# A gate matrix written by accumulating scatters in place of one-hot products, in a PEER expert layer

## The reference

```
qry = (xt @ w_query).reshape(PEER_BLOCK, PEER_HEADS, 2, PEER_KEY_DIM)
s1, s2 = scores of the two halves of qry against keys1, keys2      # 128 each
v1, i1 = lax.top_k(s1, PEER_TOPK);  v2, i2 = lax.top_k(s2, PEER_TOPK)
cand_s = all 16 x 16 sums v1 + v2;  top_s, pos = lax.top_k(cand_s, PEER_TOPK)
idx = i1 * 128 + i2 of the chosen pairs
gate = softmax(top_s)
act = gelu(einsum('td,thkd->thk', xt, expert_u[idx]))
out = einsum('thk,thkd->td', gate * act, expert_v[idx])
```

## Time and profile before

| what | us |
|---|---|
| median of 3 runs | 4345.73 (4339.46 to 4351.4) |
| the profiled execution, its own time | 4333.4 |
| span of that execution, first to last instruction | 4331.6 |
| PE busy | 3828.7 |
| DVE busy | 2677.1 |
| POOL busy | 1476.8 |
| ACT busy | 911.4 |

### The profile page before, as it was taken

The page is one execution under the profiler, slowest core; times in us unless marked ns, Lnnn a source line. Parts: engine busy times, 40 slices in busy tenths (PEclk is TensorE's granted clock), DMA queues, the critical chain, the costliest instruction groups (busy, mean ns, idle before and its releaser), DMA issues. The chain is left out here.

```text
span 4331.6 us, 43998 instructions
## 1 busy us (share of the span) xinstructions
PE 3828.7 (88%) x16016; PEld 2836.8 (65%) x16016; DVE 2677.1 (62%) x5272; ACT 911.4 (21%) x1953; POOL 1476.8 (34%) x1456
## 2 busy tenths in 40 slices
PE   8889999967999999994798899999669999999937
PEld 7647788856766666651685478788557666666516
DVE  4865116568567666777658651175685676667775
ACT  2252202146200000000123522021461000000001
POOL 6102000023355455556370020000243555555663
PEclk9899999989999999997898999999899999999968
DMA  3001233358899999999620102333589999999996
GB/s 101 30 32 37 84 136 119 125 191 285 338 391 399 405 391 410 375 410 401 252 80 30 39 30 94 126 127 133 192 292 348 388 402 404 391 410 374 409 384 258
DMA packets 300550, 1063.83 MB, mean 246 GB/s; under 512 B 41648, under 2 KB 75056, under 8 KB 274992
## 3 DMA queue, kind: packets, MB, share of 16 engines
q0 software_dynamic: 147456, 536.94, 32.2%
q1 hardware_dynamic: 119312, 488.44, 29.6%
q10 hardware_dynamic: 33568, 35.65, 2.3%
HBM read 1025.27 MB, written 35.65 MB: 245 GB/s over the span
## 5 line engine op out<-in xcount | busy, mean ns | idle before, releaser
L2022 POOL DMA_INDIRECT u_rows<-in_peer_u,idx_all x512 | 659.1, 1287 | 1654.8 <-DVEq L1925 933.5
L1629 PE MATMUL bank<-v_tile,shared 128*128 128x512 f32 x2048 | 904.5, 596 | 15.3 <-DVE shared L1972 15.2
L1945 DVE SCALAR_TENSOR_TENSOR x<-v_rows,act_w,x 128x1024 f32<-128x1024 f32 x512 | 657.7, 1285 | 210.8 <-DMA v_rows<-in_peer_v,idx_all 180.7
L2022 POOL DMA_INDIRECT v_rows<-in_peer_v,idx_all x512 | 582.3, 1137 | 456.1 <-DVE x L1945 340.9
L1629 PEld LDWEIGHTS bank<-v_tile,shared 128*128 128x128 f32 x2048 | 391.5, 191 | 466.9 <-issue 443.0
L1933 DVE CUSTOM_DVE_ANT_0 u_rows<-u_rows,h 128x1024 f32<-128x1024 f32 x512 | 606.4, 1224 | 103.3 <-DMA u_rows<-in_peer_u,idx_all 102.2
L1617 PE MATMUL bank<-hT,bT 128*128 128x256 f32 x2048 | 452.5, 379 | 0.0
L1617 PEld LDWEIGHTS bank<-hT,bT 128*128 128x128 f32 x2048 | 388.4, 190 | 72.0 <-issue 22.0
L1520 PE MATMUL bank<-hT,ring 128*128 128x256 f32 x1536 | 340.9, 383 | 14.2 <-PEq L150 14.2
L1520 PEld LDWEIGHTS bank<-hT,ring 128*128 128x128 f32 x1536 | 293.5, 192 | 56.5 <-issue 15.8
L1799 ACT ACTIVATE shared<-bank 128x512 f32<-128x512 f32 x128 | 76.2, 595 | 1023.4 <-PE bank L1629 948.7
(11 more groups left out here) (356 smaller groups left out, 5143.9 us busy)
## 6 DMA issues: line engine op xcount, KB each, us to landing
v_tile<-in_peer_v SPq DMA_DIRECT2D x256, 512.0 KB, 7.1
ring<-in_w_in_panels SPq DMA_DIRECT2D x76, 1024.0 KB, 4.8
bT<-in_peer_ut SPq DMA_DIRECT2D x128, 512.0 KB, 7.5
ring<-in_peer_w_query SPq DMA_DIRECT2D x32, 1024.0 KB, 4.9
aT<-in_peer_ut SPq DMA_DIRECT2D x64, 512.0 KB, 6.7
sT<-in_peer_ut SPq DMA_DIRECT2D x64, 512.0 KB, 7.1
gates<-dense_gates SPq DMA_DIRECT2D x32, 1024.0 KB, 10.6
ring<-in_ple_w_gate SPq DMA_DIRECT2D x24, 1024.0 KB, 7.9
```

The lines of the kernel that those rows point to most:

```text
L1629: ins = mm(acc[t][part][:, :], act_pair[p % AHEAD][:, at:at + P], v_tile[:, e % DENSE, part * 512:part * 512 + 512], start=(e == 0), stop= ...
L1945: stt(out=m.x[:, 2 + t, :], in0=vr[:, n % RINGS, :], scalar=act_w[:, p % 4, i:i + 1], in1=m.x[:, 2 + t, :], op0=ALU.mult, op1=ALU.add).the ...
L2022: nc.gpsimd.indirect_dma_start(out=rows[:, n % RINGS, :], out_offset=None, in_=table, in_offset=bass.IndirectOffsetOnAxis(ap=idx_all[:, t, ...
```

## The change

The `hot` steps and `slots` are gone. The gates are put into the DRAM matrix one by one instead.

In `phase_attend`, POOL sets a tile of zeros and SP issues 8 DMAs of 2 MB that clear this layer's cells; SP waits for them before the phase ends. In `choose`, for the first half, DVE computes the flat number of the cell (second index, first index, token) with two fused instructions and a conversion; `token` (two columns of token numbers) is made by three small DVE instructions at the start of the tail. For each head, POOL issues 32 indirect DMAs (`scatter`) of 128 single elements, each of which adds its element to its cell (`compute_op=ALU.add`), 256 in a layer. Several heads of one token can choose the same cell, so POOL waits for all adds of one head to land before it issues those of the next. Seven heads' adds come before the first fetch in POOL's program, the last head's 32 lie among the fetches of chunks 0 to 3, eight to a chunk. SP waits for all 256 before it reads the first gates.

The order changes too: four `pre` pairs come before chunk 0, two more before each of chunks 0 to 3; `values` is spread over chunks 5 to 55, and `DENSE_END` is 56. The layout of a token's cells in DRAM loses its blocks of 32 tokens; each read of the gates is as large as before.

```diff
 # phase_attend, SP
             Panels(m, s, []).stream(sp, input_panels(io, layer, "deltanet"))
+            sp.wait_ge(s.zeros_set, 1)
+            n = KEYS // ZERO_PARTS
+            for k in range(ZERO_PARTS):
+                sp.dma_start(io.gates[layer, :, n * k:n * (k + 1), :].rearrange("p e t -> p (e t)").rearrange("p (r z) -> p r z", z=ZEROS),
+                             over(zeros[:, :].unsqueeze(1), (P, n * HALF_T // ZEROS, ZEROS))).then_inc(s.cells_cleared, 16)
+            sp.wait_ge(s.cells_cleared, 16 * ZERO_PARTS)
...
 # tail_order
-    pairs = 0
-    for q in range(QUADS):
-        order.append(("hot", q))
...
-    for c in range(HOT_CHUNKS, CHUNKS + 2):
-        goal = min(PAIRS_ALL, -(-(c - HOT_CHUNKS + 1) * PAIRS_ALL // (DENSE_END - HOT_CHUNKS)))
+    for c in range(CHUNKS + 2):
+        order += [("pre", p) for p in range(UPFRONT + 2 * c, min(UPFRONT + 2 * c + 2, AHEAD))]
+        goal = max(0, min(PAIRS_ALL, -(-(c - VALUES_FROM + 1) * PAIRS_ALL // (DENSE_END - VALUES_FROM))))
...
 # SP, values(0)
-                    for k in range(2):
-                        sp.wait_ge(stored[k], 16 * 4)
+                    sp.wait_ge(m.scattered, 16 * SCATTERS * PEER_HEADS * (layer + 1))
...
 # DVE, choose, part 3, first half of the tokens
+                        step.step(stt(out=chosen[:, 0], in0=chosen[:, 0], scalar=float(HALF_T), in1=over(token.unsqueeze(2), (P, 2, TOPK)),
+                                      op0=ALU.mult, op1=ALU.add))
+                        step.step(stt(out=chosen[:, 0], in0=chosen[:, 1], scalar=float(KEYS * HALF_T), in1=chosen[:, 0], op0=ALU.mult, op1=ALU.add))
+                        step.mark(ts(cell_all[:, :, some], chosen[:, 0], float(layer * CELLS), None, ALU.add))
...
 # POOL
+            def scatter(n):
+                t, col = n % SCATTERS // TOPK, n // SCATTERS * TOPK + n % TOPK
+                if n % SCATTERS == 0:
+                    pool.wait_ge(s.first_chosen, n // SCATTERS + 1)
+                    if n:
+                        pool.wait_ge(m.scattered, 16 * (SCATTERS * PEER_HEADS * layer + n))
+                nc.gpsimd.indirect_dma_start(
+                    out=cells, out_offset=bass.IndirectOffsetOnAxis(ap=cell_all[:, t, col:col + 1], axis=0),
+                    in_=cell_gate[:, t, col:col + 1], in_offset=None, compute_op=ALU.add,
+                ).then_inc(m.scattered, 16)
+
+            late = SCATTERS * (PEER_HEADS - 1)
+            for n in range(late):
+                scatter(n)
             for n in range(RINGS):
                 fetch(n, s.u_free, u, tables[0], m.u_landed)
...
+                if c < LATE_CHUNKS:
+                    for n in range(SCATTERS // LATE_CHUNKS):
+                        scatter(late + c * SCATTERS // LATE_CHUNKS + n)
```

More of the change, by code:

```diff
@@ L710, in _ @@
             Panels(m, s, []).stream(sp, input_panels(io, layer, "deltanet"))
+            sp.wait_ge(s.zeros_set, 1)
[4 more added lines that the diff above has]
+            sp.wait_ge(s.cells_cleared, 16 * ZERO_PARTS)
+        @block.gpsimd
+        def _(pool):
+            nc.gpsimd.memset(zeros[:, :], 0.0).then_inc(s.zeros_set, 1)
         @block.scalar
@@ L1315 @@
 AHEAD = 12
-EARLY = 6
-STORE_T = 32
-BLOCKS = HALF_T // STORE_T
+ZEROS = 512
+ZERO_PARTS = 8
 OCT = 8
 OCT_PAIRS = OCT // 2
-QUADS = HALF_T // 4
-HOT_CHUNKS = 8
-DENSE_END = 58
+CELLS = P * KEYS * HALF_T
+SCATTERS = 2 * TOPK
+LATE_CHUNKS = 4
+UPFRONT = 4
+VALUES_FROM = 5
+DENSE_END = 56
 def tail_order():
@@ L1347, in tail_order @@
     order += [("choose", PEER_HEADS, part) for part in range(4)]
-    order += [("score", 1, 1), ("slots",)]
+    order += [("score", 1, 1)] + [("pre", p) for p in range(UPFRONT)]
     beside = {}
@@ L1587, in score @@
                 ins.then_inc(s.act_filled, 1)
[L1589 to L1605, removed]
             def pre(p):
@@ L1662, in embedded @@
                 ins.then_inc(s.vec_filled, 1)
-            parts = {"gate": gate, "mix": mix, "out": out, "norm": norm, "query": query, "score": score, "slots": slots, "hot": hot, "pre": pre,
+            parts = {"gate": gate, "mix": mix, "out": out, "norm": norm, "query": query, "score": score, "pre": pre,
                      "values": values, "turn": turn, "embedded": embedded}
@@ L1750, in score @@
                 elif half or head >= 4:
-                    act.wait_ge(s.dsel_ready, head + 5 if half else head - 3)
+                    act.wait_ge(s.first_chosen, head + 5 if half else head - 3)
                 bank = banks.take()
@@ L1823, in _ @@
             parts = {"gate": gate, "mix": mix, "norm": norm, "query": query, "score": score, "choose": choose, "chunk": chunk,
-                     "slots": slots, "hot": hot, "pre": pre, "embed": embed, "turn": turn, "embedded": embedded}
+                     "pre": pre, "embed": embed, "turn": turn, "embedded": embedded}
             for what, *n in order:
@@ L1833, in _ @@
             tt, ts, stt = nc.vector.tensor_tensor, nc.vector.tensor_scalar, nc.vector.scalar_tensor_tensor
+            spread = hit[:, 0:KEYS // TOPK, :].rearrange("p a n -> p (a n)")
+            step.mark(tt(spread, m.c("ident"), m.c("iota"), ALU.mult))
+            step.settle()
+            step.mark(nc.vector.tensor_reduce(token[:, 0:1], spread, AX_X, ALU.add))
+            step.settle()
+            step.mark(ts(token[:, 1:2], token[:, 0:1], float(P), None, ALU.add))
+            step.settle()
             def mix(half, pair):
@@ L1917, in choose @@
                     for a in range(2):
-                        step.mark(nc.vector.tensor_reduce(chosen[:, a] if half else dsel[:, a, :, some], h5[:, a], AX_X, ALU.add))
+                        step.mark(nc.vector.tensor_reduce(chosen[:, a], h5[:, a], AX_X, ALU.add))
                     v.wait_ge(s.exp_done, 2 * k + 2)
@@ L2003, in embedded @@
                 tt(xs, xs, ple_sig[:, n, at].rearrange("p (t c) -> p t c", t=len(UNITS[unit])), ALU.add).then_inc(s.ple_added, 1)
-            parts = {"mix": mix, "out": out, "norm": norm, "choose": choose, "chunk": chunk, "hot": hot, "values": values, "add": add,
+            parts = {"mix": mix, "out": out, "norm": norm, "choose": choose, "chunk": chunk, "values": values, "add": add,
                      "embed": embed, "turn": turn, "embedded": embedded}
```

80 lines of the change are left out of this document (18 added, 62 removed).

## The result

The changed kernel takes 4609.8 us (median of four runs, 4609.2 to 4614.6) and the kernel before 4347.4 (four runs, 4339.5 to 4351.4): a ratio of 1.061, 95% interval 1.059 to 1.063. It is 262 us slower. The forecast was 4289, and the range ended at 4560.

What follows compares the result with a forecast made beforehand. PE and DMA were taken as full together from 1160 to 1900 us, with slack only before `values`. Starting `values` 59.5 us earlier minus 31 for moved chunks gives 28.5 per layer, 57 in both: 4289 us, range 4225 to 4560.

Steps and rivals of the forecast that it cites:

- The step that failed: POOL's adds: each priced like an indirect fetch, one every 1.24 us in the choosing stage, 1.49 in the chunks.
- POOL's start: Choosing stage, layer 1: head 0 ready at 682.9 plus about 0.6 us of new DVE instructions, so adds start at 683.5.
- 224 adds to the first fetch: Seven heads of 32 adds on POOL, 42.7 us each with landing, put the first fetch at 982.4 instead of 919.77.
- From the first fetch to the last add: POOL in chunks 0 to 3: 70 fetches and adds at 1.49 us, 104.3 us, to 1086.7.
- From there to the product: Landing 3 us, gates to DVE's product 5.5, PE 1.3 later, 3 for lower clock: `values` starts at 1099.5.
- Rival (a): Adds cost POOL more than fetches; gain gone at 1.35 us, with 0.47 us more busy time 4529 us; chance 0.30.
- The landing: POOL's wait behind each head for its last add to land before the next head: taken as 3 us.
- The end: Dense stretch and behind: three chunks, 12.6 MB, move into full DMA time, costing 31 us per layer of the 59.5 gained.
- The clearing: Attention stage: clearing writes 16.8 MB, needs 42 us at 397 GB/s, covered by some 120 us of idle DMA; cost nothing.
- (c): Dense stretch: the three chunks cost 17 us each, giving back 51 of 59.5 us per layer; 4329 us; chance 0.14.
- (d): Layer's end: gain kept in full, extra chunk hidden and the rest where PE idled 52.94 us; 4227 us; chance 0.12.
- (b): DMA engines drain adds slower than POOL issues them, 1.36 us each, perhaps 2.7; about 5030 us; chance 0.06.

Runs made afterwards that it cites:

- forms kernel: A kernel of its own, POOL issuing 24 indirect DMAs of each form and none of the layer's work: median 1549 ns with the add flag, 962 without.
- the split kernel: Against the kernel before: tile 0's gates by adds, tile 1's by `hot` steps; 4273.3 us, ratio 0.983; three variants moved `DENSE_END` or the start of `values`, 4219.7 to 4247.5.
- a spacer: Changed kernel with single-element gathers in place of adds, plus a POOL memset of 384 columns behind each gather: 4440.3 us, ratio 1.021.

## Why the prediction was wrong

**The step that failed** is "It also handles 128 rows, so the nearest row is the fetch, and I take 1.24 us for it". The nearest row was near in what POOL handles and not in how. The add takes 1.55 us and 0.30, 1.85 in place of 1.24. The forms kernel shows the 0.59 by itself, whatever is moved, and the runs with half of the adds and with none show what it does. The prediction's terms for the start of `values` against the trace of after:

- POOL's start: 683.5 predicted, 686.85 measured: +3.3. Of that 2.9 is there before the choosing: the DeltaNet phase's first product starts at 259.27 in place of 256.39.
- 224 adds to the first fetch: 298.9 us predicted (982.4 - 683.5), 444.9 measured: +146. Of that 224 x (1.85 - 1.24) = 137 is the form; the landings took 14 beyond the usual gap (15.8 us in six waits) in place of 7 x 3 = 21; of the other 17, 6 are adds longer than 1.55 us and most of the rest four gaps of 1.9 to 3.2 us for which the profile names no releaser.
- From the first fetch to the last add: 104.3 predicted, 117.1 measured: +13, which is 32 adds by 0.3 to 0.4 each.
- From there to the product: 12.8 predicted, 14.2 measured: +1.4. From the last add to the read of the gates 1.4 us, where I had 3; from there to DVE's product 6.4, where I had 5.5; and PE 6.4 behind it, where I had 1.3 and 3, since the first `v_tile` loads stand behind SP's new wait, which I left out.

Together +163.5: 1263.0 in place of 1099.5. In the kernel as a whole the adds come to 487 us, the difference to the kernel without them.

**Rival (a)** names the mechanism and its break-even, 1.35 us, and the prediction's own test ("If the adds are 1.4 us apart or more") decides it. It had 0.30, and its price was a guess: 0.47 us more busy time, where the mean of 1.60 is 0.66 more. With that, 4289 + 512 x 0.66 = 4627, 17 over what was measured. The upper bound of the add, 2.18, was sound and its end, 4770, was named; the range was then cut at 4560 because the fetch seemed near. There the range failed, not at the bound.

**What the sum did not ask** is how many adds fit. It had POOL behind DVE by its own numbers, the first fetch at 982.4 against 919.77, and charged that; but it took all 256 adds of a layer as given. The first 128 cost 14 us a layer and the other 128 cost 229; this is what the split kernels use.

**The landing** is near: the waits behind a head are 2.28 us at the border shown above and 2.45 on average, where I took 3. The Trainium skill, "DMA: Bandwidth & Descriptors", "Anatomy of one DMA — SWDGE (gpsimd) path", has a fixed 2.0 us for the setup and completion of a DMA. By that figure, 32 adds issued 1.85 us apart and done one after the other would leave 32 x 0.15 + 2.0 = 6.8 us behind a head (an estimate). The measured 2.45 bears out the overlap.

**The end** is right in size and half right in reason. By the bytes the three chunks were to cost 31 us per layer; the tail grew by 35.9, from 1013.3 to 1049.2, and in every kernel with after's order it is within about 2 us of that (1047.1, 1050.3, 1048.8), wherever `values` started. But the split kernel has a tail of 1045.7 with the dense result added after chunk 56 and 1027.9 after 58, with the same bytes. So there about half of the term comes with the edit of `DENSE_END`, which the prediction counted as one chunk beside the products and two behind them, at no extra price. That after itself would gain as much by it was not run.

**The clearing** at nothing holds nearly. It is visible where it should be, the DMA share in 130:250 rose from 0.03 to 0.39, and PE was busy 99.3 us there against 98.5. The next phase began 2.9 us later than before (259.27), but in the four split kernels, which clear half as much, it began at 255.9 to 260.9, so a cost of the clearing is not told from the scatter between runs. POOL's start 3.3 us later than predicted takes in whatever it costs in the first layer.

**Rivals (c) and (d)** had no chance to show once (a) was true. (b) is out: the DMA engines drain the adds as POOL issues them, with 2.45 us of waiting behind a head. Its packets were right and its price was not. The software queue of after, and under it that of the kernel with plain scatters (packets, MB, share):

```profile
q0 software_dynamic: 221184, 537.23, 34.3%
```

```profile
q0 software_dynamic: 163840, 537.23, 30.4%
```

Against the 147456 of before an add leaves 144 packets, as many as a fetch, and a plain scatter of single elements 32. From 980 to 1120 us of after, where only adds run, the DMA share is 0.23; at one add in 1.85 us that is an estimate of 0.43 us of each engine, where (b) had 1.36 and more.

**What stays open** is the slowdown with single-element transfers 1.25 us apart. Shown is that it comes with gathers and with scatters, that it is gone with a spacer and 1.55 us between them, and that in it PE waits for nothing that the profile names. Which resource the engines share is not shown. Whether adds at a fetch's price would have met it no run can show, as an add always takes 1.55 us; the plain scatter, which has that price, is 5% slower than before. So no run reaches 4289 with all 256 transfers in a layer, and that the price of the instruction alone stood in the way is not shown.

## What to carry to other kernels

An engine's price for an instruction form is that of the form with its flags, not of a relative with the same number of rows: if no row of the trace has the form, a kernel of 24 in a row gives it (though not what the form does to other engines at work), and without that the range must reach to the bound. When work moves to an idle engine, ask first how many instructions fit before the engine is next needed; here the first 128 adds a layer cost 14 us and the next 128 cost 229, and the kernel that gave POOL only what fits and left the rest where it was is 2.7% faster than before. And read the end of a stage by a fixed mark: the tail from the first product to the next phase told apart what the start and what the order of the chunks cost.

## What the hardware showed that was not expected

- An indirect DMA with the add flag takes POOL 1.55 us for 1, 16 or 1024 elements a row alike, and 1.42 over 64 partitions; without the flag it takes 0.95 to 0.96, for 1 or 1024 elements.
- An add of 128 single elements leaves 144 packets on the DMA engines, a plain scatter or gather of them 32.
- Single-element indirect transfers issued 1.25 us apart without a pause, gathers or scatters, slow PE, DVE and ACT to about half or less (PE: 314 to 327 products in 183 us against 746 to 758) some 15 us after they begin. At 1.55 us, with a memset of 0.44 us behind each, there is nothing of it, and the kernel is 122 us faster.
- The DMA engines were not full in that time: their share was 0.15, less than the 0.37 with the spacer.
